# Reordering the seam between the two token passes of the embedding at the end of a hybrid decoder layer

## What is computed

```
h = h + (p_l @ w_ple) * sigmoid(rmsnorm(h, g_ple) @ w_ple_gate)
y = rmsnorm(h, g_final)
```

## Time and profile before

| what | us |
|---|---|
| median of 3 runs | 2149.03 |
| the profiled execution | 2154.25 |
| its span, first to last instruction | 2152.5 |
| TensorE busy | 2062.1 (96%) |
| VectorE busy | 871.7 (40%) |
| ScalarE busy | 437.5 (20%) |
| GpSimd busy | 636.8 (30%) |

### The profile page before, as it was taken

The page is one execution under the profiler, slowest core; times in us unless marked ns, Lnnn a source line. Parts: engine busy times, 40 slices in busy tenths (PEclk is TensorE's granted clock), DMA queues, the critical chain, the costliest instruction groups (busy, mean ns, idle before and its releaser), DMA issues. The chain is left out here.

```text
span 2152.5 us, 35295 instructions
## 1 busy us (share of the span) xinstructions
PE 2062.1 (96%) x12956; PEld 2006.1 (93%) x12956; DVE 871.7 (40%) x1447; ACT 437.5 (20%) x839; POOL 636.8 (30%) x417
## 2 busy tenths in 40 slices
PE   7999999999999899995998999999999999999997
PEld 7999999988988899995898989999999999999997
DVE  4111444443465355562557333312311421344556
ACT  4112333311111222222122122101200200221212
POOL 5233223222222212221233323233323332333434
PEclk9999999999999999997899999999999999999999
DMA  7321112143533344535453411111111111111313
GB/s 189 89 80 46 59 46 63 50 124 86 148 103 84 117 129 143 164 122 177 137 165 97 145 32 49 49 49 40 48 49 49 40 48 49 49 41 47 98 50 128
DMA packets 245619, 186.97 MB, mean 87 GB/s; under 512 B 15778, under 2 KB 218602, under 8 KB 245420
## 3 DMA queue, kind: packets, MB, share of 16 engines
q1 hardware_dynamic: 236140, 167.02, 26.9%
q10 hardware_dynamic: 9408, 18.99, 2.4%
HBM read 151.88 MB, written 34.12 MB: 86 GB/s over the span
## 5 line engine op out<-in xcount | busy, mean ns | idle before, releaser
L143 PE MATMUL acc<-x_hi,w_hi 128*128 128x344 f32 x2496 | 816.5, 327 | 15.4 <-PEq L1552 6.9
L143 PE MATMUL acc<-x_hi,w_lo 128*128 128x344 f32 x2496 | 802.2, 321 | 0.0
L143 PE MATMUL acc<-x_lo,w_hi 128*128 128x344 f32 x2496 | 802.2, 321 | 0.0
L113 POOL TENSOR_SCALAR w_hi<-w_raw 128x1024 fp32r<-128x1024 f32 (+1 forms) x176 | 184.4, 1048 | 1300.8 <-PE acc L143 1044.6
L143 PEld LDWEIGHTS acc<-x_hi,w_hi 128*128 128x128 f32 x2496 | 474.1, 190 | 25.1 <-issue 18.7
L143 PEld LDWEIGHTS acc<-x_lo,w_hi 128*128 128x128 f32 x2496 | 473.9, 190 | 2.2 <-issue 2.2
L143 PEld LDWEIGHTS acc<-x_hi,w_lo 128*128 128x128 f32 x2496 | 473.6, 190 | 0.0
L116 POOL TENSOR_TENSOR w_lo<-w_raw,w_hi 128x1024 fp32r<-128x1024 f32 (+1 forms) x176 | 406.8, 2311 | 14.7
L143 PE MATMUL acc<-z_hi,w_hi 128*128 128x344 f32 x768 | 246.6, 321 | 0.0
L143 PE MATMUL acc<-z_hi,w_lo 128*128 128x344 f32 x768 | 245.6, 320 | 0.0
L143 PE MATMUL acc<-z_lo,w_hi 128*128 128x344 f32 x768 | 245.5, 320 | 0.0
(11 more groups left out here) (302 smaller groups left out, 2138.0 us busy)
## 6 DMA issues: line engine op xcount, KB each, us to landing
w_raw<-in_w_in SPq DMA_DIRECT2D x64, 512.0 KB, 4.4
page<-in_cache_k SPq DMA_DIRECT2D x64, 256.0 KB, 2.9
v_page<-in_cache_v SPq DMA_DIRECT2D x64, 256.0 KB, 2.7
w_raw<-in_w_up SPq DMA_DIRECT2D x32, 512.0 KB, 4.1
w_raw<-in_w_down SPq DMA_DIRECT2D x32, 512.0 KB, 3.8
merge_gate<-merge_gates SPq DMA_DIRECT2D x24, 516.0 KB, 3.9
merge_gates<-gate_out ACTq DMA_DIRECT2D x16, 516.0 KB, 3.3
w_raw<-in_w_ple_gate SPq DMA_DIRECT2D x16, 512.0 KB, 3.8
```

Source lines behind the costliest of these rows:

```text
L113: nc.gpsimd.tensor_scalar(k.w_hi[:, par, 0:kb, :], k.w_raw[:, par, 0:kb, :], 1.0, 1.0, ALU.mult, ALU.mult).then_inc(k.w_rounded, 1)
L143: mm = k.nc.tensor.matmul(k.acc[:, c, 0:CW], w[:, par, i, :], x[:, i, cols], start=(i == 0 and j == 0), stop=(i == kb - 1 and j == 2))
```

## The change

Three engines get another order from the second block of the first pass on; nothing is added or taken away. On TensorE gates 16 goes in front of embed 14 and 15, gates 17 in front of embed 16 and the token sums, and in the second pass each embedding goes behind the gates of the next unit, with the transposes of a tile in front of these gates. On VectorE both additions of a pair go first and both sums of squares follow (for m from 2 on); in the second pass both outputs of a tile come first, then the scaling of the new unit, then addition and sum of the unit before. ScalarE follows the same order.

```diff
--- before.py
+++ after.py
@@ -1995,20 +1995,21 @@
                     gates(2 * m + 1)
                     embed(2 * m - 2)
                     embed(2 * m - 1)
+                gates(NE)
                 embed(NE - 2)
                 embed(NE - 1)
-                for m in range(KD):
+                gates(NE + 1)
+                embed(NE)
+                pe.wait_ge(s["sq_summed"], NE)
+                token_sums(range(EARLY_TILES))
+                for m in range(2, KD):
+                    for e in range(2):
+                        if m > 2:
+                            pe.wait_ge(s["y_ready"], 2 * m - 5 + e)
+                        turn_half(pt[:, e, :], m - 2, range(4 * e, 4 * e + 4)).then_inc(s["half_turned"], 1)
                     gates(NE + m)
-                    if 1 <= m <= EARLY_TILES:
-                        for e in range(2):
-                            j = 2 * m - 2 + e
-                            if j >= 2:
-                                pe.wait_ge(s["y_ready"], j - 1)
-                            turn_half(pt[:, e, :], m - 1, range(4 * e, 4 * e + 4)).then_inc(s["half_turned"], 1)
-                    embed(NE + m)
-                    if m == 0:
-                        pe.wait_ge(s["sq_summed"], NE)
-                        token_sums(range(EARLY_TILES))
+                    embed(NE + m - 1)
+                embed(NG - 1)
                 a, b_ = EARLY_TILES, EARLY_TILES + 1
                 pe.wait_ge(s["added"], NG - 1)
                 pe.wait_ge(s["produced"], NG - 1)
@@ -2156,25 +2157,28 @@
                 for m in range(2, KD):
                     scale_gate(2 * m)
                     scale_gate(2 * m + 1)
-                    for u in (2 * m - 2, 2 * m - 1):
-                        add_gated(u)
-                        add_squares(u)
-                for u in (NE - 2, NE - 1):
-                    add_gated(u)
-                    add_squares(u)
-                for m in range(KD):
-                    u = NE + m
-                    scale_gate(u)
-                    early = 1 <= m <= EARLY_TILES
-                    if m == 1:
-                        dve.wait_ge(s["gain_in"], 16)
-                        dve.wait_ge(s["n3_ready"], 1)
-                    if early:
-                        early_output(2 * m - 2)
-                    add_gated(u)
-                    if early:
-                        early_output(2 * m - 1)
-                    add_squares(u)
+                    add_gated(2 * m - 2)
+                    add_gated(2 * m - 1)
+                    add_squares(2 * m - 2)
+                    add_squares(2 * m - 1)
+                scale_gate(NE)
+                add_gated(NE - 2)
+                add_gated(NE - 1)
+                add_squares(NE - 2)
+                add_squares(NE - 1)
+                scale_gate(NE + 1)
+                add_gated(NE)
+                add_squares(NE)
+                dve.wait_ge(s["gain_in"], 16)
+                dve.wait_ge(s["n3_ready"], 1)
+                for m in range(2, KD):
+                    early_output(2 * m - 4)
+                    early_output(2 * m - 3)
+                    scale_gate(NE + m)
+                    add_gated(NE + m - 1)
+                    add_squares(NE + m - 1)
+                add_gated(NG - 1)
+                add_squares(NG - 1)
                 dve.wait_ge(s["n3_ready"], 2)
                 dve.wait_ge(s["half_turned"], 2 * EARLY_TILES + 1)
                 for i, banks in ((EARLY_TILES, (k.acc[:, 2, :], pt[:, 0, :])), (EARLY_TILES + 1, (k.acc[:, 0, :], pt[:, 1, :])),
@@ -2259,15 +2263,17 @@
                     open_gate(2 * m + 1)
                     squares_of(2 * m - 2)
                     squares_of(2 * m - 1)
+                open_gate(NE)
                 squares_of(NE - 2)
                 squares_of(NE - 1)
-                for m in range(KD):
-                    u = NE + m
-                    open_gate(u)
-                    if m == 1:
-                        token_root(0, ((slice(0, EARLY_TILES), P),))
-                        act.preload_act_table_set("sigmoid_and_others")
-                    squares_of(u)
+                open_gate(NE + 1)
+                squares_of(NE)
+                token_root(0, ((slice(0, EARLY_TILES), P),))
+                act.preload_act_table_set("sigmoid_and_others")
+                for m in range(2, KD):
+                    open_gate(NE + m)
+                    squares_of(NE + m - 1)
+                squares_of(NG - 1)
                 token_root(1, ((slice(EARLY_TILES, TB), P), (slice(TB, NTILE), B)))
     k.blocks = e0 + 2 * KD
```

## The result

| | before | after |
|---|---|---|
| median of 17 runs each | 2150.37 us | 2155.46 us |
| ratio, 95% interval | | 1.0024 [1.0016, 1.0031] |
| profiled execution, its span | 2154.25, 2152.5 | 2155.46, 2153.7 |

The change makes the kernel about 5.1 us slower (interval 3.4 to 6.7). The forecast was 0.8 us slower, with the range up to 2153.2.

The account below looks back on a forecast made before the run. TensorE, busy 96% of the span, was taken as the bound. Terms +0.2 - 0.1 + 0.6 = +0.7, rounded up to +0.8, on the median of 2149.03 gave 2149.8 us, range 2145.5 to 2153.2.

Parts of the forecast that it names:

- step (4): Clock after the single wait before the token sums: low clock costs 1.65 us, same as before, bounds 0 and 2.0.
- step (6): Second pass, five rounds from gates(18): TensorE waits 0.8 us for outputs instead of 0.9; -0.1 us, bounds 0 and +4.
- (1) to (3): Between the passes: first wait goes, splits 10 and 11 precede token sums, which start 3.1 us later after 4.25 idle.
- one sign of being right: VectorE before the token sums: a sum of about 2.7 us beside w_lo 11.
- (5): From token sums up to gates(18) and embed(17): done at 2117.95 where it was 2117.7, +0.2 us.
- (7): Tail after gates(23): two embeddings follow instead of one, late transposes wait for addition 22; +0.6 us, bounds 0 and 1.4.
- the slower one: Second pass becomes VectorE's: sums behind w_lo, outputs behind the sum, rounds of 5.44 us; 2153.5 us, chance 0.14.
- The signs of being wrong: Token sums at or before 2107.3, or TensorE waiting over 3 us for second-pass outputs, or for w_lo.

Follow-up runs that it names:

- Experiment 2: Kernel after, with GpSimd's split of weights 11 held back until the sums of squares of unit 15 are in; ratio to before 1.0009.
- experiment 1: Kernel after, with 32 extra matmuls that nobody reads between embed(16) and the token sums; ratio to before 1.0003.
- Experiment 3: Kernel after, with each second-pass sum of squares put behind the two outputs of the next round on VectorE; ratio to before 1.0014.
- experiment 12: Kernel after, with split 11 held back and the second-pass squares behind the outputs, no extra matmuls; ratio to before 1.0003.
- experiments 5: Kernel before, with only the change's second part: gates(17) in front of embed(16) and the token sums, and the new second pass; ratio to before 1.0008.
- 10: Kernel before, with the 8 transposes of tile 0 moved in front of gates(17), straight behind the token sums; ratio to before 1.0011.
- 11: Kernel before, with gates(17) ahead of embed(16) and token sums, new second pass, squares behind outputs, embed(22) ahead of gates(23); ratio to before 0.9995.

## Why the prediction was wrong, by its steps

The means of the three executions are 49.5 and 53.2 us: 3.7 more, where the sum was +0.7. Of the missing 3.0, 1.3 lie in step (4) and 1.5 in step (6).

- **(1) to (3), right, but for the order inside split 11.** The first wait goes, splits 10 and 11 fall on the additions and sums, one idle piece is left. Additions 14 and 15 were held and not sum 14, so one sign of being right, the sum of 2.7 us beside w_lo 11, is missing; the token sums come at the forecast time even so. Forecast: token sums 3.1 us later than before, idle 4.25; measured 3.4 (15.68 - 12.30) and 4.15. The Trainium skill (SBUF — State Buffer, Who interferes with whom) has one instruction hold the port for its whole length; the trace agrees, with 4.07 us for two sums that need 1.2 alone, the second ending 0.41 us behind w_lo. Experiment 2 shows the part of split 11: 2.2 us.
- **(4), mis-sized.** Forecast 1.65 us for the low clock, bounds 0 and 2.0; measured 3.6, 2.7 and 2.6. Token sums, transposes and gates(18) took 8.73, 7.84 and 7.77 us in the three executions, 5.2 at full clock in experiment 1. The bound came from a row that I had cut at 4.00 us, and I didn't ask how long the clock stays down there. The trace of before has it: TensorE waits 5.02 us, not 4.00, and the clock is low from 1280.1 to 1286.6, of which 5.44 us are work.

```profile
1281.16 3.78 PE L1896 MATMUL n_sums<-sq_sum,ones 128*128 128x344 f32 x6 [5.02 <-PEq L1674]
```

```profile
1280.10:1286.60 6.50, 5.44 (x13) 4.06 (x14) 0.74 (x1) 4.40 (x7) 0.06 (x1) 0.50 0.50 136
```

Read to its end that row gives 2.7 us, which is what two of the three executions lose. In all three the clock falls inside the wait of 4.15 us, and the work behind it then runs low for the rest of 6.8 or 10.2 us.
- **(5), right but for that.** Without the clock term (experiment 1) gates(18) ends where it was reckoned, to 0.4 us.
- **(6), the failed step.** Forecast -0.1: TensorE would wait for outputs 0.8 us in all. The five rounds to gates(23) took 24.9 us (2116.12 to 2141.02), 2.4 more than TensorE's own 22.5, and before 23.45: **+1.45**. The mechanism stood in the text, but as the rival: a sum behind w_lo, both outputs behind the sum. It held in all but the first rounds (5.2, 5.15 and 5.35 us for the last three, TensorE's own work being 4.5). w_lo held three of the sums for 2.05 us each and once the addition (2.25 us at 2122.57). I had counted late loads as relief. In this trace they were none: split 14 starts only at 2127.02, when its load has landed, and the sum of that round is held all the same.

```profile
2127.02 1.05 POOL L113 TENSOR_SCALAR w_hi<-w_raw 128x1024 fp32r<-128x1024 f32 x1 [2.49 <-DMA w_raw<-in_w_ple_gate]
2128.15 2.45 POOL L116 TENSOR_TENSOR w_lo<-w_raw,w_hi 128x1024 fp32r<-128x1024 f32 x1
```

```profile
2128.84 2.05 DVE L2131 TENSOR_TENSOR final_sums<-final_sums,ple_prod 128x264 f32<-128x264 f32 x1 [0.49 <-ACT ple_prod L2239]
```

Experiment 3 shows it: 2.3 us back, with no wait for an output left.
- **(7), right.** From the end of gates(23) to the last token sums 4.62 us, forecast 4.75, with the wait for addition 22 (0.32 us).

Of the rivals, the slower one (2153.5) was nearest, and had 0.14. It and the forecast are not alternatives: the transition and the second pass lose separately, and the low clock comes on top. The signs of being wrong did not catch this: TensorE waited 2.4 us for outputs, under the 3 that I had named.

The result lies 5.7 us above the forecast of 2149.8. The two steps account for 2.9. Another 1.3 is no step of the working: the kernel before has a median of 2150.37 in 17 runs, where the forecast stood on 2149.03 from 3. The remaining 1.4 is open. The difference of the traces put on 2149.03 would give 2152.8, inside the range.

The timed difference is 5.1 us, that of the traces 3.7, within the interval (3.4 to 6.7). The traces of all twelve experiments also come out more favourable than their ratios, by 0.1 to 2.7 us, all but 12 within the intervals. That all lean one way speaks against chance, and the profiles don't say where such a rest would lie: ahead of embed(12) TensorE takes the same 84.4 us, behind the last token sums 7.9 to 8.1. It stays open. Why the same seam has the clock low for 3.4 us once and 6.8 us another time (2 and 12), or 6.8 and 10.2 (after), is open too.

## What to carry to other kernels

A product that is moved forward also moves what waits for it: here GpSimd's splits, which then hold VectorE's additions of two SBUF operands in front of the one wait that counts. Price the low clock behind a merged wait by rows on how long it stays low, not by the idle time. Put operations that can be held by GpSimd behind those that TensorE waits for: that alone gave 2.3 us of stretch here.

## Not expected of the hardware

Less idle time does not mean a shorter stretch at the low clock. 4.08 us in two pieces were followed by 3.4 us at 0.50 in three executions of before, the first of these pieces (2.78 us) by 3.4 us already in experiments 5, 10 and 11, one piece of 1.97 us (with 0.38 ahead of it) by 6.8 us in experiment 2 and by 3.4 in experiment 12, and 32 matmuls that nobody reads, in a wait of 4.15 us, by none at all.
